# One decode-and-prompt step of a two-layer hybrid decoder: the mLSTM's convolution and gates beside the input projection, weights in single tiles, a state ring of ten tiles

## What is computed

```python
def causal_dwconv(x, buf, w, b):                  # width 4
    xp = jnp.concatenate([buf, x], axis=1)
    y = b
    for j in range(CONV_W):
        y = y + w[j] * xp[:, j:j + L]

# RG-LRU, layer 0
a = jnp.exp(log_a)
b = jnp.sqrt(-jnp.expm1(2.0 * log_a)) * (i * xf)

# mLSTM, layer 1
xm, z = jnp.split(xn @ w_in, 2, axis=-1)          # 1024 -> 2 x 2048
xc = jax.nn.silu(causal_dwconv(xm, conv_buf, conv_w, conv_b)[0])
q, k, v = block_diag(xc, wq), block_diag(xc, wk), block_diag(xm, wv)
gates = jnp.concatenate([q, k, v], axis=-1) @ w_gate + b_gate
i_pre, f_pre = gates[..., :NH_C], gates[..., NH_C:]
h, C, n, m = mlstm_chunkwise(q, k, v, i_pre, f_pre, C0, n0, m0)   # C0: 8 x 4 heads of 512 x 512
y = (rms(h) * norm_w + skip * xc) * jax.nn.silu(z)
return y @ w_out
```

## Time and profile before

| | us |
|---|---|
| median of 3 runs (lowest, highest) | 1373.2 (1372.6, 1373.51) |
| the profiled execution, its own time | 1377.05 |
| its span in the profile | 1375.3 |
| busy: TensorE, VectorE, ScalarE, GpSimd | 1161.0, 692.3, 529.1, 140.6 |
| chain that ended last: TensorE, VectorE, DMA | 73%, 11%, 7% |
| bytes moved | 260.75 MB, mean 190 GB/s |

### The profile page before, as it was taken

One profiled execution on the slowest core, in us unless ns is written; L12 is line 12 of the kernel. 1 busy time (PEld: TensorE's weight loads), 2 busy tenths in 40 slices (PEclk: granted clock), 3 DMA queues, 4 the chain that ended last, 5 costly groups with the idle time before them and its releaser, 6 DMA issues.

```text
span 1375.3 us, 21469 instructions
## 1 busy us (share of the span) xinstructions
PE 1161.0 (84%) x8297; PEld 993.4 (72%) x8297; DVE 692.3 (50%) x958; ACT 529.1 (38%) x851; POOL 140.6 (10%) x208
## 2 busy tenths in 40 slices
PE   3999865556589699999799978989998797999995
PEld 3999622245489599999789955545463787999995
DVE  4444547531123744434476954657576437554343
ACT  5333132521124555434344653425241345554331
POOL 3000000000001222100150031000000012221000
PEclk9999877767879799999989987989897797999998
DMA  6543558858823244534343222979788642443430
GB/s 246 184 173 139 203 212 308 292 196 322 300 99 136 77 166 173 183 123 183 122 154 130 115 93 92 329 275 363 274 312 320 224 176 70 176 180 126 168 138 34
DMA packets 68873, 260.75 MB, mean 190 GB/s; under 512 B 8068, under 2 KB 9284, under 8 KB 60872
## 3 DMA queue, kind: packets, MB, share of 16 engines
q1 hardware_dynamic: 68808, 259.85, 52.5%
HBM read 218.10 MB, written 41.73 MB: 189 GB/s over the span
## 4 chain that ended last, share of the span: by engine, by line
PE 73%; DVE 11%; DMA 7%; ACT 4%; issue 2%; SPq 2%; POOL 1%; POOLq 0%; DVEq 0%; ACTq 0%
PE ps L1617 18%; PE ps L1619 18%; PE ps L1618 18%; DMA kv_c<-in_kv 5%; PE ps L1978 3%; DVE cring L1410 2%; PE ps L1975 2%; PE ps L1950 2%; PE ps L1744 1%; PE ps L1853 1%; PE ps L1845 1%; DVE x L1055 1%; SPq L519 1%; PE ps L1665 1%; DVE xin_lo L1034 1%
## 5 line engine op out<-in xcount | busy, mean ns | idle before, releaser
L1004 DVE TENSOR_TENSOR w_lo<-w_raw,w_hi 128x1024 fp32r<-128x1024 f32 x232 | 283.8, 1227 | 201.0 <-ACT w_hi L633 200.7
L1617 PE MATMUL ps<-xin_hi,w_hi 128*128 128x288 f32 x1088 | 334.2, 307 | 52.4 <-DVE xin_lo L1034 29.3
L633 ACT ACTIVATE w_hi<-w_raw 128x1024 fp32r<-128x1024 f32 x232 | 243.0, 1055 | 236.6 <-PE ps L1619 224.7
L1618 PE MATMUL ps<-xin_lo,w_hi 128*128 128x288 f32 x1088 | 327.6, 301 | 0.0
L1619 PE MATMUL ps<-xin_hi,w_lo 128*128 128x288 f32 x1088 | 326.5, 300 | 0.0
L1617 PEld LDWEIGHTS ps<-xin_hi,w_hi 128*128 128x128 f32 x1088 | 210.0, 193 | 60.8 <-issue 41.5
L1618 PEld LDWEIGHTS ps<-xin_lo,w_hi 128*128 128x128 f32 x1088 | 211.2, 194 | 0.5
L1619 PEld LDWEIGHTS ps<-xin_hi,w_lo 128*128 128x128 f32 x1088 | 211.4, 194 | 0.0
L1617 PE MATMUL ps<-hid_hi,w_hi 128*128 128x288 f32 x512 | 152.4, 298 | 5.7 <-POOL hid_lo L1527 5.7
L1618 PE MATMUL ps<-hid_lo,w_hi 128*128 128x288 f32 x512 | 151.8, 296 | 0.0
L1619 PE MATMUL ps<-hid_hi,w_lo 128*128 128x288 f32 x512 | 151.3, 295 | 0.0
(11 more groups left out here) (364 smaller groups left out, 1716.7 us busy)
## 6 DMA issues: line engine op xcount, KB each, us to landing
w_raw<-in_weights SPq DMA_DIRECT2D x58, 2048.0 KB, 7.9
cring<-in_C SPq DMA_DIRECT2D x64, 512.0 KB, 6.2
out_Cs<-cring SPq DMA_DIRECT2D x64, 512.0 KB, 4.9
kv_a<-in_kv SPq DMA_DIRECT2D x64, 448.0 KB, 5.7
kv_b<-in_kv SPq DMA_DIRECT2D x32, 448.0 KB, 6.1
kv_c<-in_kv SPq DMA_DIRECT2D x32, 448.0 KB, 7.1
out_Cp<-cring SPq DMA_DIRECT2D x8, 512.0 KB, 5.0
x<-in_x SPq DMA_DIRECT2D x1, 1152.0 KB, 5.0
```

The source lines that it names most:

```text
L633: act.activation(w_hi[:, l % UM], w_raw[:, u % 2, l % UM], ACT.Copy).then_inc(hi_ready, 1)
L1004: dve.tensor_tensor(w_lo[:, l % UM], w_raw[:, u % 2, l % UM], w_hi[:, l % UM], ALU.subtract).then_inc(lo_ready, 1)
L1617: pe.matmul(ps[:, j, 0:T], w_hi[:, j, ws], hi, start=start and kk == 0, stop=False)
L1618: pe.matmul(ps[:, j, 0:T], w_hi[:, j, ws], lo, start=False, stop=False)
```

## The change

1. **Weights in single tiles.** `w_raw` has eight slots of one tile, each with a semaphore and a 512 KB load; `w_lo` is written over the `w_raw` tile that it comes from. A slot is loaded again when the step that used it is done (`step_done`), no longer when its rest is made (`lo_ready`). The 16 KB per partition that this frees ("spare") hold four `kv` slots, so all eight are loaded at the program's start, and the first four `cring` slots.
2. **RG-LRU.** The argument of the root is made as `(a*a + 1) * tanh`, from `rp` and `tp`; the reciprocal is gone.
3. **`IN_C`** is written out step by step: convolution of block `g-4` in step `g` on VectorE; the gate matmuls behind step 21, their sum behind step 22, ScalarE's parts in steps 23 to 28, VectorE's chain in step 26 (counting from 0), the transposes behind step 30. ScalarE makes the sample copy `xms`. Three memsets (`gate_zeros`) stand ahead of VectorE's loop. GpSimd makes head 0's `bd` after step 25.
4. **Samples in thirds.** `samples_thrice` makes the three copies by 12 matmuls of 32 rows into three row groups, in place of 4 of 96 rows; `xcs3` and `xms3` are gone.
5. **State ring.** Ten slots, loads eight items ahead; four items are loaded before `IN_C`'s own weights. `bd` is two tiles over the weight slots. SiLU of `z` is made per head (`b == 2`).
6. **Back to `OUT_C`.** Tiles 0 and 1 are loaded from item 54 on, 2 and 3 when the last old-state product is made, 4 to 6 after the last outer product, 7 after slot 6's last store; ScalarE waits for the last stores of the slots that lie in `w_hi` and in the input's place.

```diff
+W_SLOTS = 8
+G_PARTS = 22
-C_SLOTS = 8
+C_SLOTS = 10
+C_EARLY = 4
...
+        w_raw, o = at("w_raw", o, W_SLOTS, TILE)
+        w_lo, _ = at("w_lo", w_raw_at, W_SLOTS, TILE, dt=F32R)
...
+            def weight_rounds(a, b):
                 with sp.Fori(a, b) as i:
-                    for s in range(2):
-                        sp.wait_ge(lo_ready, UM * (2 * i + s - 1))
-                        unit(2 * i + s, s)
+                    for s in range(W_SLOTS):
+                        sp.wait_ge(step_done, W_SLOTS * i + s - W_SLOTS + 1)
+                        weights(W_SLOTS * i + s, s)
...
+            for i in range(C_EARLY):
                 c_load(i)
+            weight_rounds(STEP0[IN_C] // W_SLOTS + 1, STEP0[OUT_C] // W_SLOTS)
+            sp.wait_ge(step_done, STEP0[OUT_C])
+            for i in range(C_EARLY, C_SLOTS - 2):
+                c_load(i)
...
             for i in range(NH * ITEMS):
+                if i == (NH - 1) * ITEMS:
+                    sp.wait_ge(stage_full, use(NH - 2, "vs") + 1)
+                    weights_back(0, 1)
                 if i == NH * ITEMS - 2:
-                    unit_back(0)
+                    sp.wait_ge(hs_psum, NH)
+                    weights_back(2, 3)
...
-                order.after(dve.tensor_scalar(hp[:, :, PAD:ROW], tp[:, :, PAD:ROW], 1.0, None, ALU.add))
-                order.after(dve.reciprocal(hp[:, :, PAD:ROW], hp[:, :, PAD:ROW]))
-                dve.scalar_tensor_tensor(tp[:, :, PAD:ROW], tp[:, :, PAD:ROW], 2.0, hp[:, :, PAD:ROW],
-                                         ALU.mult, ALU.mult).then_inc(b_arg, 1)
+                order.after(dve.tensor_tensor(hp[:, :, PAD:ROW], rp[:, :, PAD:ROW], rp[:, :, PAD:ROW], ALU.mult))
+                dve.scalar_tensor_tensor(tp[:, :, PAD:ROW], hp[:, :, PAD:ROW], 1.0, tp[:, :, PAD:ROW],
+                                         ALU.add, ALU.mult).then_inc(b_arg, 1)
...
+            gate_zeros()
+            for g in range(UM * UNITS[IN_C]):
+                if base + g + 2 not in STOPS:
+                    dve_lo(g + 2, 0, base)
+                if 0 <= g - 4 < CT:
+                    conv_rest(g - 4)
+                if g == G_PARTS:
+                    rows_to_store()
+                if g == G_PARTS + 2:
+                    forget_abs()
+                if g == G_PARTS + 4:
+                    gate_chain()
+                dve.wait_ge(step_done, base + g + 1)
+                dst_c(0, g % 8, g)
...
+            def samples_thrice(h, name, i, lhs):
+                out = staged(h, name)
+                for e in range(ET):
+                    for r in range(3):
+                        last = pe.matmul(out[NS * r:NS * r + NS, P * e:P * e + P], lhs(ET * h + e),
+                                         weights_of(h, i, e), start=True, stop=True, skip_group_check=True)
+                last.then_inc(stage_full, 1)
```

More of the change, by code:

```diff
@@ L338, in program @@
         consts_c_in = sem("consts_c_in")
[L339 removed]
+        raw_in = [sem(f"raw_in{s}") for s in range(W_SLOTS)]
         hi_ready = sem("hi_ready")
@@ L525, in _ @@
                 const(dst, name)
-            unit(0, 0)
-            unit(1, 1)
+            for s in range(W_SLOTS):
+                weights(s, s)
             sp.wait_ge(lruw_zero, 1)
@@ L1618, in step @@
                     pe.matmul(ps[:, j, 0:T], w_hi[:, j, ws], lo, start=False, stop=False)
-                    last = pe.matmul(ps[:, j, 0:T], w_lo[:, j, ws], hi, start=False, stop=stop and kk == UK - 1)
+                    last = pe.matmul(ps[:, j, 0:T], w_lo[:, l % W_SLOTS, ws], hi, start=False, stop=stop and kk == UK - 1)
                 last.then_inc(step_done, 1)
@@ new lines, in gate_sum, with gate_columns @@
+            def gate_sum():
+                pe.wait_ge(gparts_copied, 1)
+                pe.matmul(ps[0:GH, 4, 0:T], gsel, gparts, start=True, stop=True).then_inc(g_ready, 1)
+            def gate_columns():
+                pe.wait_ge(gact, 3)
+                four = ident[0:NH, 0:NH]
+                for tt in range(2):
+                    for i, src in enumerate((gg_c, gw_c)):
+                        c0 = 2 * NH * tt + NH * i
+                        pe.transpose(ps[:, 5, c0:c0 + NH], src[:, P * tt:P * tt + P], four)
+                pe.transpose(ps[0:NS, 5, 4 * NH:5 * NH], gg_c[:, SEQ:T], four)
+                pe.transpose(ps[0:NS, 5, 5 * NH:6 * NH], rows[:, R_ENS:R_ENS + NS], four)
+                pe.transpose(ps[0:3 * NS, 5, 6 * NH:7 * NH], gw_c[:, SEQ:SEQ + 3 * NS], four).then_inc(gcol_ready, 1)
@@ new lines, in _ @@
+            for g in range(UM * UNITS[IN_C]):
+                step(IN_C, STEP0[IN_C] + g, g, lambda kk: (xin_hi[:, kk], xin_lo[:, kk]), True, True,
+                     (lambda kk: pe.wait_ge(xin_ready, 2 * MT + kk + 1)) if g == 0 else None, OUT0[IN_C] + g)
+                if g == 0:
+                    mean(4)
+                if g == G_PARTS - 1:
+                    gate_products()
+                if g == G_PARTS:
+                    gate_sum()
+                if g == G_PARTS + 8:
+                    gate_columns()
```

370 lines of the change are left out of this document (173 added, 197 removed).

## The result

| | before | after |
|---|---|---|
| median (lowest, highest), us | 1372.9 (1369.11, 1373.51), 4 runs | 1358.56 (1357.52, 1361.85), 4 runs |
| ratio, 95% interval | | 0.9887 [0.9865, 0.9909] |
| profiled execution, own time; span | 1377.05; 1375.3 | 1361.85; 1360.0 |
| both once more, later | 1373.3, 11 runs | 1359.96, 6 runs, ratio 0.990 [0.988, 0.992] |

The forecast was 1353.8 (1347 to 1364) with 0.94 for faster. The kernel is 14.3 us faster where 19.4 were forecast. Between the two profiled executions it is 15.2 us. One execution in this document, of the variant in experiment 4 with the reciprocal back, was in a slower state of the chip and is left out of its numbers.

A forecast was written before the change was run, and what follows sets the result against it. TensorE was taken to bound the dense layers' steps, with VectorE as full late in `IN_C`. Terms -11.1 + 1.0 + 0.5 - 3.3 - 2.2 - 3.1 - 1.2 = -19.4 gave 1353.8 us from the median 1373.2, range 1347 to 1364.

The forecast's parts named there:

- Gates moved: Gate work moved into `IN_C`'s steps: 16.0 us leave the path, TensorE pays 4.9 there, net -11.1.
- The memsets: Three memsets ahead of VectorE's loop in `IN_C`, where TensorE waits for the third tile's rest: +1.0 us.
- the chain's +0.5: VectorE's chain in `IN_C`, delayed 1.0 us by GpSimd's diagonals with 0.5 of room: +0.5, ends 0 and 3.9.
- Exponentials, transposes, clock of the prologue: Between `IN_C`'s last step and head 0's scores and values: -16.0 gates, -3.3 exponentials and transposes, -2.2 clock.
- the 16.0 that I took off: Stretch from `IN_C`'s last step to head 0's queries (convolution, gate matmuls, sum, biases, logarithms), claimed to leave the path.
- The clock's -2.2: Head 0's queries, keys, scores and values near head 1's speed without long holes: -2.2 us, ends 0 and -3.3.
- RG-LRU: -3.1 forecast: Without the reciprocal the second half ends 7.3 us sooner, the sample softmax's exponential 3.1 sooner; ends -2 and -4.
- the named end with late masks: Lower end of the gain at the sample softmax, -2 us, if masks requested amid cache transfers land late.
- thirds side by side: Twelve small sample matmuls at each of eight places run side by side across row groups: 0 us.
- rival (a): Half of the side gains lost: chain +3.4, low prologue clock +2.2, late masks +1.1; 1360.5 us, chance 0.15.
- the bound of 14: Forecast wrong if the stretch from `IN_C`'s last step to the scores, 34.2 us before, shrinks by less than 14.
- Two signs were to show the forecast wrong: `IN_C` steps spaced above 3.2 us, or a head taking over 60 us.

The follow-up runs named there:

- experiment 4: Reciprocal put back into the changed kernel: 1363.5 us, ratio 0.9928; the new root argument alone in the kernel before: 1369.9 us, ratio 0.9964.
- experiment 5: Changed kernel with the twelve small sample matmuls ordered one row group after another, not in turn: 1368.7 us, ratio 0.9966.

## Why the prediction was right, and where it was off

**Gates moved: right in kind, 2.8 us too good in `IN_C`.** By the distances of the `z` rows around them (7.5, 4.0 and 3.8 us where a step takes 3.2) the gate matmuls cost 4.3, the sum 0.8 and the transposes 0.6: 5.7 for 4.9. The memsets cost 0.9 for 1.0. *The step that failed is the chain's +0.5*: the hole measured 2.3, and 2.6 with the slower matmuls right behind it. I had priced GpSimd's 12 diagonals from the nearest row and taken one delay and a half. That part was nearly right (0.9 for 1.0). The memset of `qz1`, which the change puts right behind them, was not in the list of what stands beside the chain, and it cost 2.0. With 0.5 us of room nothing could absorb it. "SBUF — State Buffer" of the Trainium skill, section "Who interferes with whom", which I weighed for the diagonals, says that a copy can enter a mode that takes the port pair shared with GpSimd, and that the later of the two is then blocked for the whole of the other's instruction. The copy's row agrees in its end, 0.03 us after the memset's. Its start, 788.11, lies within the last diagonal and 0.28 ahead of the memset's, so the rows don't show that it was the later of the two. For the instructions with two inputs the delay was 0.03 to 0.21 us each, not the diagonals' whole 4.4.

**Exponentials, transposes, clock of the prologue: -21.5 forecast, -20.2 measured.** The exponentials and transposes left as said. Queries, keys and scores ran at the full clock. The missing 1.3 us are in my reading of the rows. The queries' row at 815.11 counts 12 instructions of 16. The other four had already run in the wait ahead of it:

```profile
809.00 1.24 PE L1845 MATMUL ps<-xcc,bd 128*128 128x288 f32 x4
```

These 1.24 us lay inside the 16.0 that I took off, and they came back to the path. The clock's -2.2 also had a share of the scores, which run from this line's end on.

**RG-LRU: -3.1 forecast, 3.5 to 5 measured** in the times of two experiments, whose intervals also hold 3.1, and 5.9 in the profile. The last rest came 7.24 us sooner for 7.3. The copies of the transposed values started at 270.79 for 270.4, and the exponential came 2.25 us sooner, near the named end with late masks, though the masks cost only 0.3 of it. What I left out is that an earlier softmax also hands cache slots back earlier; in the profile the stage's gain passed the upper end of 4, and why stays open.

**Zeros that held:** thirds side by side (experiment 5), single tiles (no engine's waits name `w_raw`, for which ScalarE waited 11.9 us before), ring of ten (six ahead is as good as eight). No run takes the single tiles or the four early items back, so that these two are worth nothing is read from the profile's waits alone. **`OUT_C`:** -1.2 forecast, -1.3 measured, behind `y_lo` without a wait for weights:

```profile
1062.63 0.60 PE L1639 MATMUL ps<-y_hi,w_hi 128*128 128x288 f32 x1 [5.42 <-DVE y_lo L1515]
```

**The heads were not zero** in the profiled execution, +2.1, with longer stretches at the lower level; in the second profile they were -0.5. And the main thing was not seen at all. The prediction called TensorE at 53.9 of 58.5 us busy the bound of a head and looked no further, while two holes of 1.4 us per head and the clock behind them were worth 20 us, more than the whole change.

**What was luck.** In the profiled pair the misses are 7.5 us of gain that did not come (`IN_C`, prologue, heads, MLP) and 3.3 us that the sum did not have, 2.8 of them at the RG-LRU. No reasoning of mine set the one against the other. Without those 2.8 us the time would stand near 1361, still in the range but with rival (a).

**Signs named ahead.** The stretch from the last step to the scores shrank by 20.2, above the bound of 14. The hole over 1.5 us did come, inside the steps and not behind them: tile 29's rest was 2.3 us late instead of 0.5. Two signs were to show the forecast wrong. In the first profile TensorE's steps keep to 3.2 us apart from the gate work, the memsets and the hole, which the sum had as terms. The third head took 60.1 us there and 60.0 in the second profile, at the bound of 60: by a hair that sign came true. Rival (a), at 1360.5, was to have the chain at +3.4 over my sum, a low clock in the prologue and late masks. The time lies nearer to it than to mine, with half of its chain term; the prologue ran at the full clock.

## What to carry over

List everything that another engine does during a chain that has little room, the clearing of a buffer too, and start such work behind the chain. In an engine that is 92% busy, look at where the other 8% lie: move work that is ready into a wait of 1.4 us before moving whole stages. Where a gain frees slots for a stage paced by transfers, carry it through to that stage's end.

## What the runs showed of the hardware

- VectorE's copy of 4x32 elements took 2.12 us beside a GpSimd memset of 1.81 us and 0.16 alone. Twelve diagonals on GpSimd took 7.05 us beside VectorE and 4.3 to 4.4 elsewhere, while the `w_lo` beside their start kept its 1.22. The side that loses need not be the one on the path.
- TensorE's granted clock fell to half in every head although TensorE was busy over 90% of the head. In head 1 of the changed kernel that was behind two holes of 1.4 us, with matmuls of one to eight columns beside it; moving work into the holes shortened the stretch from 10.8 to 7.4 us. Heads of the same code took 58.3 or 61.4 us, by one such stretch or two. Why some variants fell into the second kind and the changed kernel's two profiles did not, is open.
- Twelve matmuls of 32 rows out, 128 columns: 1.07 us when neighbours write different row groups, 2.0 when they write the same.
